# Who issues the query loads of a neighbourhood-attention loop: SyncE or ScalarE

## The reference, cut to what matters

```python
s_loc = jnp.einsum('bqhd,biqjhd->bhqij', q_row, k_win) * scale + bias
s_ctx = jnp.einsum('bqhd,bkhd->bhqk', q_row, k_ctx) * scale
s = jnp.concatenate([s_loc.reshape(...), s_ctx], axis=-1)
p = jax.nn.softmax(s, axis=-1)
out = (jnp.einsum('bhqij,biqjhd->bqhd', p_loc, v_win)
       + jnp.einsum('bhqk,bkhd->bqhd', p_ctx, v_ctx))
```

## Time and profile before

| | |
|---|---|
| time, median of 3 runs | 1681.65 us (1679.63 to 1682.25) |
| the profiled execution's own time | 1681.91 us |
| its span, first to last instruction | 1680.1 us |
| mean granted TensorE clock | 0.991 of full speed |
| PE busy | 1632.4 us (97%) |
| DVE, ACT, POOL busy | 978.7, 767.1, 185.6 us |
| DMA queue of SP (q1), of POOL (q0), of ACT (q10) | 162.41, 42.72, 4.77 MB |

### The profile page before, as it was taken

How to read it: one execution, slowest core, us unless ns; L and a number is a source line. 1 busy time by engine, 2 the same in 40 slices (tenths; PEclk the granted TensorE clock), 3 DMA queues, 4 the chain that set the end, 5 groups by cost and what they waited for, 6 DMA issues and landing times.

```text
span 1680.1 us, 22056 instructions
## 1 busy us (share of the span) xinstructions
PE 1632.4 (97%) x8706; PEld 1386.7 (83%) x8706; DVE 978.7 (58%) x1266; ACT 767.1 (46%) x1094; POOL 185.6 (11%) x226
## 2 busy tenths in 40 slices
PE   6999999999999999999999999998999999999998
PEld 6878888889898788888886888997887788888887
DVE  5355554576555467776777657537874655335543
ACT  4233433343444356565565378626872333223320
POOL 3770000000000000000000000105750000000000
PEclk8999999999999999999999999999999899999999
DMA  8552113333324244566643312488743233333332
GB/s 254 194 182 75 51 53 122 126 101 126 103 98 144 74 123 129 161 196 189 189 153 121 101 51 75 140 240 220 201 131 101 60 90 85 102 101 99 92 91 80
DMA packets 258374, 211.12 MB, mean 126 GB/s; under 512 B 7827, under 2 KB 241662, under 8 KB 258286
## 3 DMA queue, kind: packets, MB, share of 16 engines
q1 hardware_dynamic: 243662, 162.41, 33.0%
q0 software_dynamic: 11456, 42.72, 7.4%
q10 hardware_dynamic: 3168, 4.77, 0.9%
HBM read 190.25 MB, written 22.76 MB: 127 GB/s over the span
## 4 chain that ended last, share of the span: by engine, by line
PE 86%; DVE 5%; ACT 5%; POOL 1%; issue 1%; DMA 1%; POOLq 0%; DVEq 0%; ACTq 0%; SPq 0%
PE ps L1713 27%; PE ps L1715 26%; PE ps L1714 26%; DVE w_lo L1097 2%; ACT w_hi L630 2%; PE ps L2118 1%; PE ps L1846 1%; POOL sc L2265 1%; ACT mod_tmp L760 1%; PE ps L2110 1%; PE ps L2111 1%; POOL q_lo L2274 1%; PE ps L1832 0%; DMA qd<-q_scr 0%; ACT np_hi L1055 0%
## 5 line engine op out<-in xcount | busy, mean ns | idle before, releaser
L1713 PE MATMUL ps<-h_hi,w_hi 128*128 128x512 f32 x960 | 376.3, 392 | 6.0 <-DVE w_lo L1097 3.5
L1714 PE MATMUL ps<-h_lo,w_hi 128*128 128x512 f32 x960 | 374.3, 390 | 0.0
L1715 PE MATMUL ps<-h_hi,w_lo 128*128 128x512 f32 x960 | 374.2, 390 | 0.0
L1097 DVE TENSOR_TENSOR w_lo<-w_raw,w_hi 128x2048 fp32r<-128x2048 f32 (+1 forms) x136 | 293.4, 2158 | 118.6 <-ACT w_hi L630 118.4
L630 ACT ACTIVATE w_hi<-w_raw 128x2048 fp32r<-128x2048 f32 (+1 forms) x136 | 242.2, 1781 | 98.2 <-PE ps L1715 94.3
L1713 PEld LDWEIGHTS ps<-h_hi,w_hi 128*128 128x128 f32 x960 | 180.6, 188 | 44.9 <-DVE w_lo L1097 4.7
L1715 PEld LDWEIGHTS ps<-h_hi,w_lo 128*128 128x128 f32 x960 | 180.5, 188 | 37.9
L1714 PEld LDWEIGHTS ps<-h_lo,w_hi 128*128 128x128 f32 x960 | 180.7, 188 | 36.6
L1713 PE MATMUL ps<-xg_hi,w_hi 128*128 128x512 f32 x352 | 138.2, 393 | 2.4 <-DVE w_lo L1097 2.4
L1715 PE MATMUL ps<-xg_hi,w_lo 128*128 128x512 f32 x352 | 137.7, 391 | 0.0
L1714 PE MATMUL ps<-xg_lo,w_hi 128*128 128x512 f32 x352 | 137.4, 390 | 0.0
(11 more groups left out here) (338 smaller groups left out, 3100.2 us busy)
## 6 DMA issues: line engine op xcount, KB each, us to landing
mod_raw<-in_l_w_mod POOLq DMA_DIRECT2D x24, 1024.0 KB, 7.8
w_raw<-in_w_ffn_in SPq DMA_DIRECT2D x44, 512.0 KB, 4.9
w_raw<-in_l_ffn_w_up SPq DMA_DIRECT2D x44, 512.0 KB, 4.6
w_raw<-in_w_in SPq DMA_DIRECT2D x40, 512.0 KB, 5.2
w_raw<-in_l_na_w_qkv SPq DMA_DIRECT2D x24, 512.0 KB, 4.6
w_raw<-in_w_mem_kv SPq DMA_DIRECT2D x16, 512.0 KB, 3.9
masked_scr<-mb POOLq DMA_DIRECT2D x16, 384.0 KB, 3.1
w_raw<-in_w_ffn_out SPq DMA_DIRECT2D x16, 384.0 KB, 3.7
```

The costliest lines, as they stand in the source:

```text
L1097: v.tensor_tensor(wlo[s][:, 0:size], raw[s][:, 0:size], whi[s][:, 0:size].bitcast(F32), ALU.subtract).then_inc(w_lo, 1)
L1713: mm(o, w_h, x_h, start=first, stop=False, **kw)
L1714: mm(o, w_h, x_l, start=False, stop=False, **kw)
L1715: return mm(o, w_l, x_h, start=False, stop=last, **kw)
```

## The change

`load_queries` moves out of SP's part and takes the issuing engine as an argument. SP still issues the queries of heads 0, 1 and 2. The loads for heads 3 to 15, 13 pairs of DMAs, are now in ACT's stream: in step g with g+2 = 4 * head + 3, behind the exponential of g+2 and ahead of the copy of g. Buffers, sizes, semaphores and counts are the same.

```diff
+        def load_queries(eng, head):
+
+            b = head % 2
+            own, other = (slice(64 * x, 64 * x + 64) for x in (b, 1 - b))
+            src = q_scr[:, 64 * head:64 * head + 64, :].rearrange("l p n -> p l n")
+            eng.dma_start(qd[b][own, :, :].bitcast(F32), src).then_inc(qd_in[b], 16)
+            eng.dma_start(qd[b][other, 0:1, :].bitcast(F32), src[:, 0:1, :]).then_inc(qd_in[b], 16)
...
             for head in range(NA_HEADS - 2):
-                if head:
-                    sp.wait_ge(ns_ps, 4 * head + 4)
-                    load_queries(head + 2)
                 if head + 3 < NA_HEADS:
                     sp.wait_ge(ns_max, 4 * head + 4)
                     load_bias(head + 3)
...
             for g in range(NA_G):
                 if 2 < g + 2 < NA_G:
                     na_exp(g + 2)
+                head, tau = divmod(g + 2, 4)
+                if tau == 3 and 1 <= head < NA_HEADS - 2:
+                    act.wait_ge(ns_ps, 4 * head + 4)
+                    load_queries(act, head + 2)
                 act.wait_ge(np_ps, g + 1)
```

More of the change, by code:

```diff
@@ L544, in load_bias @@
                 sp.dma_start(bias[b][:, 0:3, :].rearrange("p k x -> p (k x)"), masked_scr[:, head, :]).then_inc(bias_in[b], 16)
[L546 to L552, removed]
             def load_values(a):
@@ L573, in _ @@
             sp.wait_ge(q_spill_last, 32)
-            load_queries(0)
+            load_queries(sp, 0)
             sp.wait_ge(w_lo, b + 12)
@@ L577, in _ @@
             load_bias(1)
-            load_queries(1)
+            load_queries(sp, 1)
             values_spilled(0)
@@ L584, in _ @@
             sp.wait_ge(ns_ps, 4)
-            load_queries(2)
+            load_queries(sp, 2)
             load_bias(2)
```

## The result

The changed kernel is slightly slower. Medians of 11 runs each: 1682.25 us before (1677.27 to 1684.38), 1684.24 after (1681.75 to 1688.51). The recorded ratio is 1.0022, with a 95% interval of [1.0014, 1.0029]. It is not the quotient of the medians, which is 1.0012: the loss is 2.0 us by the medians and 3.7 by the ratio, so its sign is sure and its size is not. The forecast was 1680.9 us, a gain of 0.8.

The account below looks back on a forecast made before the run. PE was taken to bound the kernel; 2.9 us gained at heads 3 and 4 and 2.1 lost to ACT's issues gave -0.8, so 1680.9 us against runs of 1681.65. The range was 1678.2 to 1685.8 us.

Parts of the forecast that it names:

- What bounds the kernel: Neighbourhood loop: PE leads; head 3's late queries cost 3.64 us, 1.85 of waiting and 1.79 of slow matmuls.
- The queries of head 3: Head 3, step 8: issued by ACT, its queries land in 6.3 us, leaving a 0.3 us stall and no clock drop.
- The queries of head 4: Head 4, where PE now arrives earlier: queries land at 1159.0, giving back up to 0.5 us, taken as 0.4.
- Onto ACT: Steps 8a+1, six even heads: ACT's two issues delay the copy 0.35 us each, 2.1 in all; odd heads nothing.
- The queries' own lateness: Even heads: queries issued 1.8 us later have 5.6 us to land, median 4.6; nothing charged.
- ACT's issue as the new bound: Even-head copies: ACT's issues delay each by 1.04 us, six times; slower, 1685.0 us; chance 0.17.
- late landings in even heads: Even heads: queries take 6.3 us and come 0.7 us late, six times; slower, 1685.0 us; chance 0.10.
- The free issue: ACT's issues delay copies 0 to 0.1 us and head 3's stall is all gone; 1678.2 us; chance 0.20.
- only issue time is saved: Head 3: queries land 1.1 us sooner, PE idles 0.75, clock drop kept; +1.0, 1682.7 us; chance 0.08.

Follow-up runs that it names:

- e10: e9 with the store of the last values' low half moved from head 1's turn to head 3's; 1678.8 us, 0.9987 against the kernel before.
- e9: e6 with the bias of head 3 issued behind the queries of head 3 instead of ahead; 1680.13 us, 1.0000 against the kernel before.
- e1: The changed kernel with only head 3's queries on ACT, SP issuing heads 4 to 15 as before; 1680.59 us, 0.9995 against the kernel before.
- e3: The changed kernel with ACT issuing all 13 loads one step earlier, behind the exponential of block 2; 1679.77 us, 0.9998 against the kernel before.
- e4: The kernel before, SP issuing everything, but from head 4 on queries wait for the maximum and go between bias and values; 1683.43 us, 1.0009.
- e5: The changed kernel with SP's values waiting until the queries have landed; 1686.04 us, 1.0034 against the kernel before.
- e6: The kernel before with the bias of head 2 loaded early, ahead of the wait for the scores; 1679.41 us, 0.9988.
- e7: e3 with e6's early bias of head 2 added; 1680.24 us, 0.9994 against the kernel before.
- e2: The changed kernel with head 3's queries left to SP, ACT issuing those of heads 4 to 15; 1686.1 us, 1.0038 against the kernel before.
- e11: The changed kernel with ACT issuing only the queries of heads 5, 7, ... 15, SP all others; 1681.8 us, 1.0010 against the kernel before.

## Why the prediction was wrong

The time, 1684.24, was inside the range, but the direction was wrong. Two steps failed: the gain at heads 3 and 4, which didn't come, and the landing of the loads of even turns, which was charged at nothing. By the prediction's own steps:

- **What bounds the kernel.** Right for that execution. Head 3's lateness was read from the earlier trace rows as 3.64 us, and e10, which removes it, has a loop 3.5 us shorter. In the medians less comes back: by its ratio e10 gains 2.2 us (0.8 to 3.7), and e9, which removes it too, nothing that can be measured. Half of the 3.64 is slow clock, which didn't follow every such wait.
- **The queries of head 3. The first step that failed.** The landing time was taken as 6.3 us, from two stores of the earlier trace rows, with 7.1 as upper bound. It was 8.9, and 10.0 in e1. A stall of 3.50 at full clock replaced 1.85 of stall and 1.79 of slow clock: 3.50 against 3.64, a gain of 0.1 where 3.3 was put. Why the stores were no measure for these loads stays open: the stores had a burst of SP beside them too. The queues before, 1118.38 to 1125.52 us, from the first store's issue to the second's landing (q1 SP's, q10 ACT's):

```profile
q1 hardware_dynamic: 2238, 1.63, 77.8%
q10 hardware_dynamic: 688, 0.67, 30.7%
```

  And after, 1142.76 to 1152.36, the same for head 3's queries:

```profile
q1 hardware_dynamic: 2478, 2.35, 87.0%
q10 hardware_dynamic: 226, 0.40, 17.9%
```

  SP's queue moved 0.23 and 0.24 MB per us, much the same; ACT's 0.09 and 0.04.
- **The queries of head 4.** 0.4 us was charged for them; PE doesn't wait for them in either kernel. The gain of the two heads together, put at 2.9 with 0.7 as the lower end, was about nothing; e1 measures 0.9995, no change. In the loop the stretch with both is 0.4 us longer. This term, 3.3 us off, is the largest error of the sum.
- **Onto ACT.** The mechanism was right, the size not: 0.35 us at each of six even places was charged, the row shows 0.10 and e3's periods 0.12. Five of them make 0.6 in place of 2.1, below the lower bound of 1.2; ACT passed the sixth, head 4's, at 1149.48, while PE stood still for head 3. I had let the issue begin after the exponential's start; it began 0.05 ahead of it.
- **The queries' own lateness. The second step that failed.** The 5.6 us available were worked out right; the landing was taken as the median, 4.6, of the earlier trace rows, and nothing was charged. It was 5.9 to 6.9. The median mixed odd turns (4.6 to 6.3) with even ones (3.1 to 4.1), and was of loads that SP had put ahead of its own burst. The loads in question would run beside it, and longer landings were already at hand: 6.03 us for head 3 in the earlier trace rows, behind values and bias, and the 6.3 that the prediction itself took for ACT's queue at heads 3 and 4. With the first the step would have charged (6.03 - 5.6) x 6 = 2.6; the runs put it at 1.9 in the loop.
- **The rivals.** What happened is the third, late landings in even heads, to which I gave 0.10, with 1685.0 us and 0.7 at six heads; it came at five, of 0.2 to 1.2. ACT's issue as the new bound is refuted by the copy's 0.10 us, where 1.04 was supposed, and by e3. The free issue was nearly true of ACT and of no use, since the stall stayed. That only issue time is saved put 0.75 us of stall at head 3; it was 3.50.

The sum as measured in the profiles: heads 3 and 4 and the rest of the first stretch +0.4 where -2.9 was put, ACT's issue +0.6 where +2.1 was, late queries +1.9 where nothing was. Together that is +2.9 in the loop, beside +2.0 by the medians and +3.7 by the ratio. That the time still fell into the range is partly luck: the issue was charged 1.5 us too much, which covered part of the other two errors.

On the rules weighed in the prediction. That all queues share the same engines (the Trainium skill, "Trainium Kernel Development and Optimization", Key Constraints) agrees with the 0.26 MB of each queue in the same 2 us; that issuing from several engines saves only issue time is too kind here, since each even load took 1.8 to 3.6 us longer to land than before. The exclusive descriptor block (the Trainium skill, "Perfetto Trace Analysis", DMA Instruction — HWDGE) doesn't show at the even place: ACT's issue at 1167.17 and SP's at 1167.16 ran together and took 0.59 and 0.33 us. It isn't excluded where SP's queue is full: beside SP's issues ACT's second query issue took 1.62 us in e1 and 1.50 in e3, at 1146.89 and 1148.86. The 763 ns that the prediction took as ACT's maximum were line 413's alone; line 414, issued by ACT beside SP's, took 1.79, 2.08 and 0.89 us before. What held them isn't shown.

In the even turns the later issue and the sharing are both needed: issued early, ahead of the values (e3), late but ahead of them in one queue (e4), and late with the values held back (e5), PE waits for at most one even load behind head 4, issued late beside them, for five. How the time divides between the two isn't settled, since e4 is too close to 1. Nor is it why head 3's load on ACT takes 9 to 10 us where the even turns' take 6 to 7. More runs beside it, as the queues show for head 6's load, 1167.17 to 1173.69 us:

```profile
q1 hardware_dynamic: 1328, 0.99, 69.8%
```

SP's queue moved 0.99 MB in 6.5 us there and 2.35 in 9.6 at head 3. But the stores of the earlier trace rows had as much beside them per us and landed sooner, so this alone doesn't explain it.

## What to carry to other kernels

A load that is issued at the last moment at which it is still harmless has a landing time of its own; moving it by one step can cost more than the issue it saves, so take its landing from a row with the same neighbours in flight, never from a median over all its places. Handing a load to an idle sequencer loses the order that one queue kept: what had been ahead of a burst can now run beside it, as in the even turns here. If one load comes late, first look at what stands ahead of it in its own queue and whether that can go earlier or later (e6 and e10; e9, with the same aim, gained nothing measurable).

## What was not expected of the hardware

An idle stretch of PE was followed by the lower clock in some executions and not in others, and its length doesn't tell which. Before: 1.85 us idle, then 0.51. After: 3.50 us, then 1.00. In e3 and e7, 1.71 and 1.59 us, then 1.00; in e2 and e11, 1.84 and 2.35 us, then 0.58 and 0.57 from 1154 to 1158. e5, after 3.40 us of idle time that ended at 1155.43:

```profile
1154.00:1156.00 2.00, 0.56 (x1) 0.50 (x2) 0.00 (x0) 0.00 (x0) 0.59 (x1) 0.50 1.09 379
```

And e1, whose idle stretch of 3.64 us ended at 1157.06:

```profile
1154.00:1158.00 4.00, 0.94 (x9) 0.82 (x10) 0.96 (x3) 0.72 (x3) 1.36 (x2) 1.00 1.08 384
1158.00:1162.00 4.00, 4.00 (x32) 3.70 (x30) 1.98 (x6) 1.96 (x4) 1.04 (x1) 0.57 1.10 287
```

The first 0.94 us of work after it still had 1.00, the next four had 0.57. So the 1.8 us that the prediction gave such a drop can neither be counted on nor excluded by the length of the wait; what decides isn't shown.
